# Rotary products of both token blocks on GpSimd, and the axial heads turned earlier, in the even mixer of a two-block transformer

## The reference, cut to what matters

```python
def even_mixer(h, w_in, q_gain, k_gain, sink, w_out, rope1, rope_axial):
    proj = h @ w_in                       # qa 512, ka 128, va 128, qb 512, kb 128, vb 128 columns
    qa = apply_axial_rope(rms_norm(qa, q_gain), *rope_axial)
    ka = apply_axial_rope(rms_norm(ka, k_gain), *rope_axial)
    oa = global_gqa(qa, ka, va)           # 8 query heads, 2 key heads, head width 64
    qb, kb = apply_rope(qb, *rope1), apply_rope(kb, *rope1)
    ob = windowed_gqa_sink(qb, kb, vb, sink)   # 8 query heads, window 128, a sink per head
    return concatenate([oa, ob]) @ w_out
```

## Time and profile before

| what | us |
|---|---|
| median of 3 runs | 1360.18 (1357.99 to 1362.19) |
| profiled execution | 1359.46 |
| its span | 1357.7 |
| TensorE busy | 1310.5 (97%) |
| VectorE busy | 953.7 (70%) |
| ScalarE busy | 731.2 (54%) |
| GpSimd busy | 147.3 (11%) |

### The profile page before, as it was taken

How to read it: one execution, slowest core, us unless ns; L and a number is a source line. 1 busy time by engine, 2 the same in 40 slices (tenths; PEclk the granted TensorE clock), 3 DMA queues, 4 the chain that set the end, 5 groups by cost and what they waited for, 6 DMA issues and landing times.

```text
span 1357.7 us, 19646 instructions
## 1 busy us (share of the span) xinstructions
PE 1310.5 (97%) x7440; PEld 1136.7 (84%) x7440; DVE 953.7 (70%) x1269; ACT 731.2 (54%) x1000; POOL 147.3 (11%) x137
## 2 busy tenths in 40 slices
PE   8999999599999999999999999999999999999995
PEld 7888887487888888888898888888889988888884
DVE  6666676868766677666676767666678778787777
ACT  6444456766444455444466666444448443556662
POOL 2200002248300000000022210000003110000000
PEclk9999999799999999999999999999999999999998
DMA  8756644046655546556554346555533343455550
GB/s 284 220 189 194 199 145 138 32 135 180 220 185 185 186 154 217 186 188 193 179 167 140 125 156 225 193 185 185 185 119 101 116 163 125 155 186 199 202 185 31
DMA packets 165426, 229.25 MB, mean 169 GB/s; under 512 B 4028, under 2 KB 135355, under 8 KB 165249
## 3 DMA queue, kind: packets, MB, share of 16 engines
q1 hardware_dynamic: 163120, 221.33, 50.3%
q0 software_dynamic: 2160, 7.24, 1.9%
q10 hardware_dynamic: 96, 0.02, 0.0%
HBM read 227.53 MB, written 1.05 MB: 168 GB/s over the span
## 4 chain that ended last, share of the span: by engine, by line
PE 84%; DVE 9%; ACT 4%; issue 2%; POOL 1%; DMA 0%; SPq 0%; DVEq 0%; ACTq 0%
PE ps L430 27%; PE ps L437 14%; PE ps L376 12%; PE ps L377 12%; PE ps L378 12%; DVE w_lo L306 3%; PE ps L675 1%; ACT w_hi L298 1%; PE ps L1379 1%; PE ps L2206 1%; POOL p_sb L1466 1%; PE ps L1342 0%; PE ps L775 0%; PE ps L543 0%; ACT p_sb L1452 0%
## 5 line engine op out<-in xcount | busy, mean ns | idle before, releaser
L306 DVE TENSOR_TENSOR w_lo<-raw,w_hi 128x2048 fp32r<-128x2048 f32 x208 | 486.0, 2339 | 98.9 <-ACT w_hi L298 98.5
L430 PE MATMUL ps<-h_both,w_hi 128*128 128x512 f32 x1744 | 418.4, 391 | 2.1 <-DVE s_sb L904 1.4
L298 ACT ACTIVATE w_hi<-raw 128x2048 fp32r<-128x2048 f32 x208 | 396.4, 1907 | 21.1 <-PE ps L378 20.6
L430 PEld LDWEIGHTS ps<-h_both,w_hi 128*128 128x128 f32 x1744 | 323.0, 188 | 67.8 <-DVE s_sb L904 1.8
L437 PEld LDWEIGHTS ps<-h_both,w_lo 128*128 128x128 f32 x1744 | 224.6, 191 | 8.9
L437 PE MATMUL ps<-h_both,w_lo 128*128 128x256 f32 x1744 | 228.1, 283 | 0.0
L898 ACT ACTIVATE s_sb<-ps 128x512 f32<-128x512 f32 x88 | 52.5, 597 | 231.2 <-PE ps L437 231.1
L376 PE MATMUL ps<-w_hi,gu_hi 128*128 128x512 f32 x400 | 156.4, 391 | 1.0 <-DVE w_lo L306 1.0
L377 PE MATMUL ps<-w_hi,gu_lo 128*128 128x512 f32 x400 | 156.2, 391 | 0.0
L378 PE MATMUL ps<-w_lo,gu_hi 128*128 128x512 f32 x400 | 155.6, 389 | 0.0
L904 DVE TENSOR_TENSOR s_sb<-ps,s_sb 128x512 f32<-128x512 f32 x88 | 60.7, 690 | 103.0 <-ACT s_sb L898 103.0
(11 more groups left out here) (344 smaller groups left out, 1679.5 us busy)
## 6 DMA issues: line engine op xcount, KB each, us to landing
raw<-in_ffn_w_up_dram SPq DMA_DIRECT2D x44, 1024.0 KB, 5.3
raw<-in_ffn_w_down_dram SPq DMA_DIRECT2D x44, 1024.0 KB, 4.9
raw<-in_ffn_w_gate_dram SPq DMA_DIRECT2D x43, 1024.0 KB, 5.4
raw<-in_w_up_dram SPq DMA_DIRECT2D x22, 1024.0 KB, 5.0
raw<-in_w_in_dram SPq DMA_DIRECT2D x14, 1024.0 KB, 5.4
raw<-in_odd_w_qkv_dram SPq DMA_DIRECT2D x12, 1024.0 KB, 5.1
raw<-in_w_down_dram SPq DMA_DIRECT2D x11, 1024.0 KB, 5.0
raw<-in_even_w_in_dram SPq DMA_DIRECT2D x4, 1024.0 KB, 5.2
```

The source lines that it names most:

```text
L298: act.activation(w_hi[slot][:, :], raw[slot][:, :], ACT.Copy).then_inc(w_hi_ready, 1)
L306: dve.tensor_tensor(w_lo[slot][:, :], raw[slot][:, :], w_hi[slot][:, :].bitcast(F32), ALU.subtract).then_inc(w_lo_ready, 1)
L430: pe.matmul(PS[:, bank, :], a[:, k, t * P:(t + 1) * P], h_both[:, :, k, :], start=k == 0, stop=False, skip_group_check=True)
```

## The change

Block 0's products go to GpSimd as well (`AXIAL_BY_POOL`). `rope_turn-2` uses banks 6, 7 and 0 in place of 0, 1 and 3, and no longer waits for `pt_lo_ready`; on TensorE it moves ahead of `turn-3`, and `scores-4` and `scores-5` each move ahead of one step. On ScalarE `exp1-4` moves ahead of `scale1-3` and `squares` ahead of the copies of pair 1; the weight splits 6, 7 and 8 come later. On VectorE `roots` and `place` move ahead of the last banded pair's inverses, and the weights' low parts 6 and 7 come later. The lists below are cut to the part that differs.

```diff
-            BANKS = (0, 1, 3)
+            BANKS = ((0, 1, 3), (6, 7, 0))
@@ pe_turn
                     pe.wait_ge(self.axial, TB)
                     pe.wait_ge(self.att.max_ready, 8)
-                    pe.wait_ge(self.att.pt_lo_ready, 8)
-                    bank = self.BANKS[slot // 2]
+                    bank = self.BANKS[n // 2][slot // 2]
@@ place
-                src = PS[:, self.BANKS[j], 0:w * S].rearrange("p (a s) -> p a s", a=w)
+                src = PS[:, self.BANKS[br][j], 0:w * S].rearrange("p (a s) -> p a s", a=w)
@@
-        AXIAL_BY_POOL = False
+        AXIAL_BY_POOL = True
@@ EVEN_TENSOR
-  scores-3 values-1 turn-2 values-2 turn-3
-  rope_turn-2 values-3 scores-4 out_first-0 scores-5 turn-4 out_second-0 scores-6 values-4 turn-5
+  scores-3 values-1 turn-2 values-2 rope_turn-2
+  turn-3 scores-4 values-3 scores-5 out_first-0 turn-4 out_second-0 scores-6 values-4 turn-5
@@ EVEN_SCALAR
-  scale1-2 axial_in-0 scale1-3 out_hi-0 exp1-4
-  hi1-2 hi1-3 exp1-5 scale1-4 scale1-5 hi1-4 exp1-6 hi1-5 out_hi-1 exp1-7 squares-0 scale1-6
-  scale1-7 hi1-6 out_hi-2 hi1-7 split_hi-6 split_hi-7 rope_hi-2 out_hi-3 split_hi-8 exp1-8 exp1-9
-  scale1-9 hi1-8 hi1-9 exp1-10 exp1-11 scale1-11 exp1-12 out_hi-4 hi1-10 hi1-11 exp1-13 scale1-13
+  scale1-2 axial_in-0 exp1-4 scale1-3
+  exp1-5 squares-0 out_hi-0 hi1-2 hi1-3 scale1-4 scale1-5 exp1-6 exp1-7 hi1-4 hi1-5 out_hi-1
+  scale1-6 scale1-7 split_hi-6 rope_hi-2 hi1-6 hi1-7 out_hi-2 exp1-8 exp1-9 out_hi-3
+  scale1-9 split_hi-7 exp1-10 hi1-8 hi1-9 exp1-11 split_hi-8 scale1-11 exp1-12 out_hi-4 hi1-10
+  hi1-11 exp1-13 scale1-13
@@ EVEN_VECTOR
-  max1-4 max1-5 out_lo-0 lo1-2 lo1-3 exp1-4 exp1-5 max1-6 axial-0 max1-7 lo1-4 lo1-5 exp1-6 exp1-7
-  roots-0 place-0 out_lo-1 lo1-6 lo1-7 split_lo-6 out_lo-2 rope_lo-2 out_lo-3 max1-8 max1-9 exp1-8
-  exp1-9 split_lo-7 max1-10 max1-11 exp1-10 lo1-8
+  max1-4 max1-5 exp1-4 exp1-5 max1-6 max1-7 out_lo-0 lo1-2 lo1-3 roots-0 axial-0 place-0 exp1-6
+  lo1-4 lo1-5 exp1-7 out_lo-1 rope_lo-2 lo1-6 lo1-7 max1-8 max1-9 out_lo-2 exp1-8 split_lo-6
+  exp1-9 out_lo-3 max1-10 max1-11 split_lo-7 exp1-10 lo1-8
@@ EVEN_GPSIMD
-  banded_q1-0 v-0 axial-1 exp1-8 exp1-10 exp1-12 exp1-14
+  banded_q1-0 v-0 axial-0 axial-1 exp1-8 exp1-10 exp1-12 exp1-14
```

More of the change, by code:

```diff
@@ L2444, in build @@
         EVEN_SCALAR = steps("split_hi-2 banded_q1-0 split_hi-3 split_hi-4 split_hi-5 kv-0 rope_hi-0 v-0 rope_hi-1 exp1-0 "
[4 rows of a table removed]
[5 rows of a table added]
                             "exp1-14 exp1-15 hi1-12 out_hi-5 hi1-13 scale1-15 out_hi-6 hi1-14 hi1-15 split_hi-9 out_hi-7 "
                             "split_hi-10 split_hi-11")
-        EVEN_VECTOR = steps("split_lo-2 split_lo-3 banded_q0-0 split_lo-4 banded_k-0 rope_lo-0 rope_lo-1 split_lo-5 max1-0 max1-1 rows-0 exp1-0 max1-2 max1-3 exp1-1 exp1-2 exp1-3 lo1-0 lo1-1 max1-4 max1-5 out_lo-0 lo1-2 lo1-3 exp1-4 exp1-5 max1-6 axial-0 max1-7 lo1-4 lo1-5 exp1-6 exp1-7 roots-0 place-0 out_lo-1 lo1-6 lo1-7 split_lo-6 out_lo-2 rope_lo-2 out_lo-3 max1-8 max1-9 exp1-8 exp1-9 split_lo-7 max1-10 max1-11 exp1-10 lo1-8 exp1-11 lo1-9 max1-12 max1-13 exp1-12 out_lo-4 max1-14 exp1-13 lo1-10 lo1-11 exp1-14 max1-15 split_lo-8 exp1-15 lo1-12 out_lo-5 lo1-13 out_lo-6 lo1-14 lo1-15 split_lo-9 out_lo-7 out-2 split_lo-10 out-3")
-        EVEN_GPSIMD = steps("banded_q1-0 v-0 axial-1 exp1-8 exp1-10 exp1-12 exp1-14")
+        EVEN_VECTOR = steps("split_lo-2 split_lo-3 banded_q0-0 split_lo-4 banded_k-0 rope_lo-0 rope_lo-1 split_lo-5 max1-0 "
[6 rows of a table added]
+        EVEN_GPSIMD = steps("banded_q1-0 v-0 axial-0 axial-1 exp1-8 exp1-10 exp1-12 exp1-14")
         ODD_TENSOR = steps("unit-0 unit-1 unit-2 scores-0 unit-3 unit-4 turn-0 scores-1 unit-5 unit-6 values-0 scores-2 "
```

## The result

The changed kernel takes 1355.74 us, the median of 13 runs (1351.54 to 1357.92), beside 1359.56 us for the kernel before in 13 runs on the same chips (1355.77 to 1362.19). The ratio is 0.9968, with a 95% interval of 0.9956 to 0.998: 4.3 us, or 0.32%, faster by the ratio, and 3.8 us by the medians. The profiled execution took 1353.35 us over a span of 1351.5, which is 6.1 and 6.2 less than before. The two gains differ because single executions of either kernel spread over some 6 us; the experiments show where a part of that spread comes from. Two executions of the kernel before, in the third group of experiments, took 3347 and 5067 us and are left out of that group's ratios.

What follows compares the result with a forecast made beforehand. Bound: serial VectorE and ScalarE work in the even mixer, paid in TensorE idle time and the half clock it leaves. Gains of 4.1 and 2.7 us sum to 6.8, giving 1353.4 us; the forecast's own range is 1350.5 to 1356.

Steps and rivals of the forecast that it cites:

- A gain of 6.8: Even mixer: 4.1 us from earlier transposes of heads 8 and 9 plus 2.7 us from the clock kept there.
- clock term: Transposes of heads 8 and 9 and the output product's second half: 3.8 us at full clock, not 6.5; 2.7 us gained.
- GpSimd's blocks: Both blocks' products on GpSimd, 5.3 us each, ending at 242.6 and 247.9; takes 2.6 us off VectorE.
- rival D: Slower: GpSimd's products and VectorE hold each other up, placing ends at 263.4, total 1364.8 us; chance 0.07.
- where the lock is paid: VectorE beside GpSimd's products: the first small root operation waits up to 0.85 us, 247.1 to 247.95.
- What is late next: First output weight's low part on VectorE now decides: output product at 264.65, transposes of heads 8 and 9 at 267.6.
- 4.1 us before the transposes: Transposes of heads 8 and 9 start at 267.6 and not at 271.73, a gain of 4.1 us.
- Rival C: Weight's low part loses the port to head 8's scaling, small stalls add up: 1354.5 to 1356.5 us; chance 0.12.
- the one of 3: Stop of 3 us around the clock's second fall; the new 2.0 us stop at 262.6 was judged shorter, so harmless.
- Rival E: The change does nothing, as the output weight's low part gates both orders at 264.7: 1358 to 1361 us; chance 0.07.

Runs made afterwards that it cites:

- the third group of experiments: Each version measured once more on one chip; the changed kernel, unedited, took 1356.61 us there, ratio 0.9974 to the kernel before.
- the two later groups: Two further measurements of the changed kernel, no edit, against the kernel before: 1356.95 us (ratio 0.998) and 1356.61 us (0.9974).
- the early split: Changed kernel with the first output weight's split moved into idle time of ScalarE and VectorE: 1353.92 us (0.9965), again 1354.4 us (0.9962).
- early fill: Changed kernel with the first output weight's split in idle time, plus idle matmuls in three early TensorE stops: 1356.1 us, ratio 0.9966.
- the banks alone: Kernel before with axial transposes in banks 6, 7 and 0 and without their wait, no queue reordered: 1358.49 us (0.9977), again 1357.27 us (0.9986).
- one filled stop (two kernels): Idle matmuls in one stop: twelve ahead of heads 8 and 9's transposes, kernel before, 1358.12 us; eight ahead of the output product, changed kernel, 1356.98 us.

## Why the prediction came out as it did

The forecast was 1353.4 us, the median 1355.74: the sign and the mechanism held, and the time lies inside the forecast's own range (1350.5 to 1356), at its upper end. A gain of 6.8 was summed. The profiled execution gave 6.1, the runs 2.7 to 4.3 by their ratios. Two things in this are luck. The close 6.1 compares a profile of before that paid the whole clock term with one of the changed kernel that paid none. And the time lies inside the range by 0.26 us only; the changed kernel's medians in the two later groups, 1356.95 and 1356.61, lie above it.

**GpSimd's blocks.** Forecast to end at 242.6 and 247.9; they end at 242.4 and 247.6. Nothing on VectorE stretched them, so rival D (slower, with placing past 258.8) had no ground: placing ends at 253.3. Its premise, that GpSimd could be stretched 2.4 times, does show up, at 2.1 times, where a weight's low part lies beside it: head 8's scaling takes 3.79 us beside the row of 263.23 and 1.83 in both profiles with the early split. The Trainium skill (SBUF — State Buffer, SBUF: two separate sides) calls this port pair an exclusive lock held for an instruction; the five pairs of equal ends above agree with it. The other page of the Trainium skill that was weighed, GPSIMD Engine Reference (Engine selection), calls GpSimd about 2x slower for such work, as it is here (5.2 us against 2.7), and would have kept the products on VectorE. By the start of the values of heads 4 and 5 that advice costs 1.8 to 1.9 us with the new order; with the old order it costs nothing by the scores of pair 6.

**The step that failed: where the lock is paid.** I charged 0.85 to the first small root operation. It paid nothing (249.30, 0.18 us), since GpSimd was done. Instead, two things came ahead of the roots. The banded inverse of head 5 took 1.47 (240.98), so that the maxima of pair 3 could not begin before 242.7, where I had 241.8; I had named that charge and not carried it into the sum. And each of these maxima ends in a small operation on two values, which the prediction left out; they took 0.78 and 0.66 where 0.23 is normal. The trace of before has a warning, in a row that the prediction doesn't use:

```profile
238.22 0.35 DVE L1435 TENSOR_SCALAR negm<-mx,neg_sink 128x2 f32<-128x2 f32 x1
```

It lay beside GpSimd's product of 238.23 and took 0.35. The reductions start at 247.74 and not at 245.5, 2.2 late; less the 0.85, what follows is 1.2 to 1.4 late up to the scores of pair 4, and 0.9 to 1.0 from the output product on: placing 251.63 (250.3), values 254.24 (253.0), axial transposes 256.97 (255.6), scores of pair 4 260.12 (258.95), output product 265.60 (264.65), transposes 268.47 (267.6). The first trace also shows a low clock in the scores of pair 3 (0.58 at 241.37), which ends them 1.3 late. The maxima did start behind them, at 243.07. But it is not the cause: in the first profile of the early split these scores ran at the high clock and the values start at 21.30 all the same; so they do, to 0.03 us, in all six profiles with both blocks on GpSimd, the new order and no early fill. What sets that time is GpSimd's queue, with VectorE in step behind it: in these six the first of the two small operations takes anything from 0.40 to 1.23 us, and the second ends 13.06 to 13.09 in every time, with GpSimd's instruction.

**What is late next.** This was the step that mattered, and it held: the low part of the first output weight takes the place of the wait that went, as the profiles of the two runs with it moved show (and their medians, by 2.2 and 3.0 us). Its high part stands earlier in ScalarE's new queue, ahead of the copies of heads 6 and 7, and not later as said ahead of the prediction; only splits 7 and 8 come later there. Of 4.1 us before the transposes, 3.2 to 3.3 came in two of the three profiles and 0.8 in the one that lost the clock. Rival C was half true. Small stalls on the way to the scores of pair 4 ate about 1 us of this term. But the weight's low part didn't lose the port to head 8's scaling: it took 2.26, as alone, and the scaling waited.

**The term that was mis-sized: the clock.** I took 2.7 with bounds of 0 and 2.7. One pair of profiles shows exactly that. But before pays 2.7 in one profile and 1.5 in the other, and the changed kernel pays nothing in two and 1.5 in a third, in the stop of 1.93 that I had set aside as too short beside the one of 3. Averaged over two profiles of before and three of the changed one, pair 6 starts 4.5 us earlier (44.6 and 40.1), not 5.9, and the medians lie about there (2.7 to 4.3). I should have priced the term over executions and not over one.

**What the parts are worth.** Rival E, that nothing changes, falls: 0.9968, 0.998 and 0.9974 all have intervals below 1. Its premise was true, as the forecast also had it: the low part gates the output product, which starts no sooner than before (32.65 against 31.77). The banks and the dropped wait alone bring 0.9977 and 0.9986, half or more of the whole by the middle values, at no cost in the queues. The rest, 0.7 us beside it on one chip, is too little to be told apart (the intervals of 0.9963 to 0.9986 and 0.9977 to 0.9996 overlap). In both profiles of the banks alone the clock is high behind the stop, in one after a stop of 2.28 us, in the other after one of 0.73 with the loss ahead of it; why, no run shows.

**What stays open.** Behind the scores of pair 7 the profiles take 1074.6 to 1080.1 us, with no order by kernel, so a single execution can't judge a change of 4 us. Why the clock fell in one execution and not in another of the same kernel, at stops of the same length, no run settles.

## What to carry to other kernels

When a change takes away a wait, look for the work that was done early and waited for by no one; here a weight's low part, moved behind the new critical work, took some 2 us of the gain, and moving it in two queues gave them back in the profiles. When work goes to GpSimd, list every VectorE operation that will run beside it, two-value ones included, and give each that can be held up the rest of a GpSimd instruction; here the adds and TENSOR_SCALARs paid, and reciprocals and reads from PSUM did not. Price a term that hangs on the granted clock by several profiles of the same kernel, and count from an event just ahead of the change. In this kernel a low clock cost time only where the work behind it wasn't waiting for another engine anyway.

## What the runs showed of the hardware

A VectorE TENSOR_SCALAR of 128x2 with both inputs in SBUF takes 0.23 us alone and up to 1.27 beside GpSimd's products (in the kernel with early fills); a RECIPROCAL of the same size stayed at 0.17, and reads from PSUM (L1432, 0.42; L1487, 0.67) were not slowed. Two scalings of 128x256 on GpSimd take 1.83 us alone and 3.79 to 3.87 beside a weight's low part on VectorE, which takes its usual 2.3. What a reduction does beside GpSimd is still not shown: no root reduction met it.

The places where the granted clock falls and rises move between executions of one kernel. Behind the same stop of 2.13 to 2.16 us ahead of the transposes of heads 2 and 3, the six profiles with the new order and no early fill show the low clock from the first of these transposes on (three of them), from within them (the first profile), from the scores of pair 3 on (one), and only behind those scores (one). The scores of pair 4 start 26.87 to 27.75 in with it. With one filled stop (two kernels) the high clock lasted through the work behind it. With three it lasted behind two of them, but was low in the values of heads 2 and 3, behind the second fill and a stop of 2.56 us, and again in those of heads 6 and 7. None of the three gained by its runs what its fills had been expected to give.
